# Second attention: value products as three one-pass products of high and low parts

## The reference, cut to what matters

```python
q = _apply_axial_rope(_rmsnorm(q, q_norm), rope)      # 512 x 8 x 128
k = _apply_axial_rope(_rmsnorm(k, k_norm), rope)      # 512 x 2 x 128
out = _blocked_attention([q], [k], v, GQA_HEAD_DIM ** -0.5)
...
s = jnp.einsum('bqkgd,bskd->bkgqs', qp, kp)
p = jax.nn.softmax(s * scale, axis=-1).astype(v.dtype)
return jnp.einsum('bkgqs,bskd->bqkgd', p, v)          # the value products
```

## Time and profile before

| | |
|---|---|
| median of 3 runs | 2506.69 us (2506.29 to 2506.73) |
| the profiled execution | 2506.91 us, span 2505.1 us |
| TensorE busy in the span | 2477.2 us (99%) |
| DVE, ACT, POOL busy | 1015.4, 1084.5, 1413.0 us |
| the second attention's phase 1 | about 2000 to 2080 us of the span |
| value products of phase 1 (L1678) | 64 records, 29.9 us busy |

### The profile page before, as it was taken

How to read it: one execution, slowest core, us unless ns; L and a number is a source line. 1 busy time by engine, 2 the same in 40 slices (tenths; PEclk the granted TensorE clock), 3 DMA queues, 4 the chain that set the end, 5 groups by cost and what they waited for, 6 DMA issues and landing times.

```text
span 2505.1 us, 36572 instructions
## 1 busy us (share of the span) xinstructions
PE 2477.2 (99%) x12648; PEld 2020.0 (81%) x12648; DVE 1015.4 (41%) x2240; ACT 1084.5 (43%) x1866; POOL 1413.0 (56%) x1100
## 2 busy tenths in 40 slices
PE   9999999999999999999999999999999999999999
PEld 7888888888888888888867688888888767888887
DVE  7567532125586652115676522111025672211100
ACT  6346552226447554225467433333144573333321
POOL 6445765566644765557734545566466264555553
PEclk9999999999999999999999999999999999999999
DMA  5312113324212112333320123333343112332332
GB/s 197 101 60 85 44 51 94 101 80 143 92 60 85 60 39 89 96 98 117 120 68 26 34 76 101 100 92 100 94 124 102 51 34 68 95 98 92 101 95 73
DMA packets 62367, 215.12 MB, mean 86 GB/s; under 512 B 7312, under 2 KB 10512, under 8 KB 61840
## 3 DMA queue, kind: packets, MB, share of 16 engines
q1 hardware_dynamic: 62224, 213.28, 27.4%
HBM read 211.16 MB, written 2.10 MB: 85 GB/s over the span
## 4 chain that ended last, share of the span: by engine, by line
PE 92%; DVE 3%; ACT 2%; POOL 1%; issue 1%; DMA 0%; SPq 0%; ACTq 0%; DVEq 0%; POOLq 0%
PE bank L873 24%; PE bank L875 24%; PE bank L874 24%; PE pair L1678 2%; PE pair L873 2%; PE pair L874 2%; PE pair L875 2%; PE bank L1743 1%; PE bank L1711 1%; PE pair L1505 1%; PE bank L1268 1%; PE pair L1281 1%; POOL wl L2596 1%; PE bank L1239 1%; PE bank L1219 1%
## 5 line engine op out<-in xcount | busy, mean ns | idle before, releaser
L2596 POOL TENSOR_TENSOR wl<-raw,wh 128x512 fp32r<-128x512 f32 x750 | 1002.5, 1360 | 867.5 <-ACT wh L2547 286.9
L873 PE MATMUL bank<-hh,wh 128*128 128x512 f32 x1600 | 632.1, 395 | 1.1 <-ACT rv L1961 0.9
L875 PE MATMUL bank<-hh,wl 128*128 128x512 f32 x1600 | 623.5, 390 | 0.0
L874 PE MATMUL bank<-hl,wh 128*128 128x512 f32 x1600 | 622.8, 389 | 0.0
L873 PEld LDWEIGHTS bank<-hh,wh 128*128 128x128 f32 x1600 | 300.5, 188 | 63.5 <-ACT rv L1961 2.7
L875 PEld LDWEIGHTS bank<-hh,wl 128*128 128x128 f32 x1600 | 300.3, 188 | 63.3
L874 PEld LDWEIGHTS bank<-hl,wh 128*128 128x128 f32 x1600 | 300.7, 188 | 59.5
L2547 ACT CAST wh<-raw 128x1024 fp32r<-128x1024 f32 x120 | 125.5, 1048 | 254.0 <-PE pair L875 140.2
L1927 ACT CAST wh<-raw 128x1024 fp32r<-128x1024 f32 x104 | 109.1, 1050 | 117.9 <-PE bank L875 92.0
L873 PE MATMUL bank<-wh,hh 128*128 128x512 f32 (+2 forms) x352 | 138.8, 394 | 2.6 <-DVE hl L2940 1.2
L2210 ACT CAST wh<-raw 128x1024 fp32r<-128x1024 f32 x84 | 86.8, 1049 | 122.1 <-PE bank L875 107.1
(11 more groups left out here) (514 smaller groups left out, 4712.3 us busy)
## 6 DMA issues: line engine op xcount, KB each, us to landing
raw<-stream SPq DMA_DIRECT2D x384, 512.0 KB, 3.6
mraw<-memin SPq DMA_DIRECT2D x3, 1024.0 KB, 5.6
par<-params SPq DMA_DIRECT2D x2, 1124.5 KB, 9.1
out<-xT SPq DMA_DIRECT2D x8, 256.0 KB, 2.0
con<-consts SPq DMA_DIRECT2D x1, 1540.0 KB, 14.9
xT<-xin SPq DMA_DIRECT2D x2, 512.0 KB, 4.6
xT<-xin SPq DMA_DIRECT2D x1, 1024.0 KB, 8.5
con<-consts SPq DMA_DIRECT2D x1, 512.0 KB, 3.2
```

Of the source, the lines that this page charges most:

```text
L873: mm(o, ah, bh, start=start, stop=False)
L874: mm(o, ah, bl, start=False, stop=False)
L875: return mm(o, al, bh, start=False, stop=stop)
L2596: m = TT(wl[slot][:, c], raw[slot][:, c], wh[slot][:, c].bitcast(F32), ALU.subtract)
```

## The change

Each turned bank is now written twice: ACT writes its high part (PTh, F32R) for all 32 tiles, and DVE the low part (PTl) for all 32, as the bank minus the high part, so DVE waits for ACT. The value tiles are split in the same way, in steps 1 (ACT, vh) and 2 (DVE, vl, in place over v). Each value product becomes a call of `three`. A turned bank is free when the low part is made. The low parts of the features of query group B move to another place, since the second set of turned probabilities needs theirs.

```diff
@@ -283,6 +283,11 @@
 
 
 PT_RING = 3
+
+
+def high_parts(m):
+
+    return 4 + NT + m + 1
 
 
 def mix_bank(e):
@@ -684,7 +689,7 @@
             b["msum"] = sb("msum_1", [P, N_MEM], at=r1 + 44 * KB_)
             b["q"] = tiles_at("q", 8, a2, dt=F32R)
             b["k"] = tiles_at("k", 2, a2 + 16 * KB_, dt=F32R)
-            b["ql"] = tiles_at("qAl", 4, r1 + 8 * KB_, dt=F32R) + tiles_at("qBl", 4, hreg + 8 * KB_, dt=F32R)
+            b["ql"] = tiles_at("qAl", 4, r1 + 8 * KB_, dt=F32R) + tiles_at("qBl", 4, r1 + 32 * KB_, dt=F32R)
             b["kl"] = tiles_at("kl", 2, a2 + 44 * KB_, dt=F32R)
             b["v"] = tiles_at("v", 4, a2 + 20 * KB_, (P, 256))
             b["qm"] = tiles_at("qm", 4, a2 + 24 * KB_)
@@ -693,8 +698,11 @@
             b["mP"], b["mPT"] = tiles_at("mP", 4, r1, (P, N_MEM)), tiles_at("mPT", 2, r1 + 4 * KB_)
             b["ra"], b["rb"] = (sb(f"{n}_1", [P, T], at=a2 + at * KB_) for n, at in (("ra", 40), ("rb", 42)))
             b["P"] = tiles_at("P", 4, hreg + 16 * KB_)
-            b["PT_sets"] = [sb(f"PT_1_{x}", [P, NT, T], at=at) for x, at in enumerate((a2 + 32 * KB_, hreg))]
-            b["PT"], b["PT_odd"] = ([s_[:, kb] for kb in range(NT)] for s_ in b["PT_sets"])
+            b["PTh"] = [sb(f"PTh_1_{x}", [P, NT, T], F32R, at=at) for x, at in enumerate((a2 + 32 * KB_, hreg))]
+            b["PTl"] = [sb(f"PTl_1_{x}", [P, NT, T], F32R, at=at) for x, at in enumerate((a2 + 24 * KB_, hreg + 8 * KB_))]
+            b["vl"] = tiles_at("vl", 4, a2 + 20 * KB_, (P, 256), F32R)
+            b["vh"] = tiles_at("vh", 4, hreg + 26 * KB_, (P, 256), F32R)
+            b["PT"] = b["PT_odd"] = b["mPT"] * 2
             b["qraw"] = sb("qraw", [P, T], at=hreg + 24 * KB_)
     ah = sb("ah", [P, FF, T], F32R, at=r1)
     al = sb("al", [P, FF, T], F32R, at=r1 + 44 * KB_)
@@ -1667,12 +1675,17 @@
                         if a + (4 if len(phases) == 2 and phase else 0) >= back and value_bank(i, phase, a) in outs:
                             pe.wait_ge(t["mix_lo"].sem, t["mix_lo"].at(a0 + a - back + 1))
                         if (i, phase) == (1, 1):
-                            pe.wait_ge(t["pt_a"].sem, t["pt_a"].at(copies_before(1, a + 1)))
-                            pe.wait_ge(t["pt_d"].sem, t["pt_d"].at(copies_before(1, a + 1)))
+                            pe.wait_ge(t["pt_a"].sem, t["pt_a"].at(high_parts(4 * a + 3)))
+                            pe.wait_ge(t["pt_d"].sem, t["pt_d"].at(high_parts(4 * a + 3)))
                         for kb in blocks:
                             copied, first = (t["pt_a"], 0) if kb < nk // 2 else (t["pt_d"], nk // 2)
                             if (i, phase) != (1, 1):
                                 pe.wait_ge(copied.sem, copied.at(copies_before(phase, a) + kb - first + 1))
+                            if (i, phase) == (1, 1):
+                                c = slice((a // 4) * P, (a // 4 + 1) * P)
+                                x = three(bk[value_bank(i, phase, a)], b["vh"][kb][:, c], b["vl"][kb][:, c], b["PTh"][a % 2][:, kb],
+                                          b["PTl"][a % 2][:, kb], kb == 0, kb == nk - 1)
+                                continue
                             vv = (b["mv"][kb][:, a * P:(a + 1) * P] if phase == 0 else
                                   b["v"][kb][:, a * P:(a + 1) * P] if i == 0 else b["v"][kb][:, (a // 4) * P:(a // 4 + 1) * P])
                             x = mm(bk[value_bank(i, phase, a)], vv, pts[a % 2][kb][:, :], start=(kb == 0), stop=(kb == nk - 1))
@@ -1732,8 +1745,7 @@
                                 pe.wait_ge(t["mix_lo"].sem, t["mix_lo"].at(4))
                         pe.wait_ge(t["p"].sem, t["p"].at(m0 + m + 1))
                         if (i, phase) == (1, 1) and m >= PT_RING:
-                            copied = t["pt_d" if (m - PT_RING) % 2 else "pt_a"]
-                            pe.wait_ge(copied.sem, copied.at(copies_before(1, 0) + (m - PT_RING) // 2 + 1))
+                            pe.wait_ge(t["pt_d"].sem, t["pt_d"].at(high_parts(m - PT_RING)))
                         elif qt == 0 and a0 + a:
                             pe.wait_ge(t["pt_a"].sem, t["pt_a"].at(copies_before(phase, a)))
                             pe.wait_ge(t["pt_d"].sem, t["pt_d"].at(copies_before(phase, a)))
@@ -2484,6 +2496,9 @@
                             if step == 16:
                                 take_root("qA")
                                 take_root("qB")
+                        elif step == 1:
+                            for x in range(NT):
+                                A(b["vh"][x][:, :], b["v"][x][:, :], ACT.Copy).then_inc(t["pt_a"].sem, 1)
                         elif step in QB_TURNS:
                             feature("qB", QB_TURNS.index(step), bk[3])
                         elif step in (12, 16, 20, 24):
@@ -2503,11 +2518,10 @@
                     pp = b["mP"] if phase == 0 else b["P"]
                     if turn and (i, phase) == (1, 1):
                         m, a, qt = turn
-                        if m % 2 == 0:
-                            act.wait_ge(t["flipped"].sem, t["flipped"].at(m0 + m + 1))
-                            if a >= sets:
-                                act.wait_ge(t["o"].sem, t["o"].at(a0 + a - sets + 1))
-                            A(b["PT_sets"][a % 2][:, :, qt * P:(qt + 1) * P], b4[m % PT_RING], ACT.Copy).then_inc(t["pt_a"].sem, 1)
+                        act.wait_ge(t["flipped"].sem, t["flipped"].at(m0 + m + 1))
+                        if a >= sets:
+                            act.wait_ge(t["o"].sem, t["o"].at(a0 + a - sets + 1))
+                        A(b["PTh"][a % 2][:, :, qt * P:(qt + 1) * P], b4[m % PT_RING], ACT.Copy).then_inc(t["pt_a"].sem, 1)
                     elif turn and turn[2] == NT - 1:
                         m, a, qt = turn
                         act.wait_ge(t["flipped"].sem, t["flipped"].at(m0 + m + 1))
@@ -3677,6 +3691,10 @@
                         if phase:
                             if step == 2:
                                 own.end()
+                                for x in range(NT):
+                                    dve.wait_ge(t["pt_a"].sem, t["pt_a"].at(4 + x + 1))
+                                    V.tensor_tensor(b["vl"][x][:, :], b["v"][x][:, :], b["vh"][x][:, :].bitcast(F32),
+                                                    ALU.subtract).then_inc(t["pt_d"].sem, 1)
                             if step in QB_TURNS:
                                 low_part("qB", QB_TURNS.index(step), bk[3])
                             return
@@ -3720,11 +3738,12 @@
                                         ALU.mult).then_inc(t["bias"].sem, 1)
                     if turn and (i, phase) == (1, 1):
                         m, a, qt = turn
-                        if m % 2:
-                            dve.wait_ge(t["flipped"].sem, t["flipped"].at(m0 + m + 1))
-                            if a >= sets:
-                                dve.wait_ge(t["o"].sem, t["o"].at(a0 + a - sets + 1))
-                            V.tensor_copy(b["PT_sets"][a % 2][:, :, qt * P:(qt + 1) * P], b4[m % PT_RING]).then_inc(t["pt_d"].sem, 1)
+                        dve.wait_ge(t["pt_a"].sem, t["pt_a"].at(high_parts(m)))
+                        if a >= sets:
+                            dve.wait_ge(t["o"].sem, t["o"].at(a0 + a - sets + 1))
+                        c = slice(qt * P, (qt + 1) * P)
+                        V.tensor_tensor(b["PTl"][a % 2][:, :, c], b4[m % PT_RING], b["PTh"][a % 2][:, :, c].bitcast(F32),
+                                        ALU.subtract).then_inc(t["pt_d"].sem, 1)
                     elif turn and turn[2] == NT - 1:
                         m, a, qt = turn
                         dve.wait_ge(t["flipped"].sem, t["flipped"].at(m0 + m + 1))
```

## The result

The changed kernel takes 2510.88 us (2510.2 to 2512.14), against 2506.71 us (2506.2 to 2507.24) for the kernel before on the same chip: a ratio of 1.0017, interval 1.0011 to 1.0023. So 4.17 us were lost; the forecast was 2511.3 us, a loss of 4.6. The prediction put at some 5.0 us what a measurement of this kernel can tell from no change; with 22 runs of each kernel a loss of 4.17 us could be told from none.

What follows compares the result with a forecast made beforehand. TensorE bound the kernel before; after the change, ACT and DVE chains would: 5.6 us late at score tile 30, less 1.0 back in value halves, +4.6 on 2506.69 gives 2511.3 us; range 2503.5 to 2515.0.

Steps and rivals of the forecast that it cites:

- The chains decide: Second attention: handovers through ACT's and DVE's in-order queues, not TensorE's work, set the pace; +4.6 us, chance 0.50.
- periods with a cast: Steps 10 to 30, four score tiles each, with one granule cast on ACT: 8.48 us against 7.96 before.
- Rival B: Second attention: handoffs are hidden and TensorE stays the bound; -1.6 us, or -5.1 if the start is absorbed; chance 0.25.
- The v copies: Start of phase, ACT: four copies between the first exponentials take 1.4 us, of which about 1.0 us delays later work.
- DVE's subtractions of v "cost nothing": Start of phase: DVE's four subtractions lie in its wait for the last memory head's mixh, adding nothing; uncovered, about 1.4 us.
- The loops: Steps 3 to 9: three two-step chains through DVE and ACT grow from 3.87 to 4.49 us, +0.62 each.
- r(10): DVE's row maximum of step 10, after the start and three loops: 2.86 us late, at 2027.29.
- T(30): TensorE's turning of score tile 30: 5.6 us late, then 1.0 us back in three shorter value halves.
- Rival C: DVE, second attention: instructions run end to end, 0.08 us more per handover; +8.0 us, 2514.7 us; chance 0.20.
- Rival D: TensorE value products: one-pass products do not follow each other by 0.23 us; at 0.28, +5.6 us, 2512.3; chance 0.05.
- The value half and TensorE's need: TensorE, two of a head's four key blocks: 1.38 us, 0.32 less; four steps then need 7.32 us.
- the case with 0.50: The forecast itself: ACT and DVE chains set the second attention's pace, +2 to +7 us; 0.20 of it above +5.0.

Runs made afterwards that it cites:

- the best order: Changed kernel with casts earlier, reciprocal before low part, v copies and subtractions spread, and low parts of steps 3, 5, 7 deferred one step: 2504.88 us, ratio 0.9993.

## Why the prediction was right, by its steps

- **"The chains decide"** held. TensorE idles (40.28 us busy, against the 43.73 of the earlier trace rows), and periods with a cast are 8.44 us with three products, one product and plain ones. Rival B is excluded by this: with one product TensorE's work is far below any chain, and the time does not follow it.
- **The v copies.** ACT's four took 1.23 us from the first start to e(2) (2008.35 to 2009.58), forecast 1.36. r(3) was 0.91 us late, forecast 1.0. By the formula of the Trainium skill (VectorE: DVE Perf Modes, The TRN2 errata) one copy is an estimate of 0.40 us; the trace agrees, with 0.41. Neighbours overlap by some 0.1 us, so four of them take 1.23 and not 1.6.
- **DVE's subtractions of v "cost nothing"** held barely, and not by the sum I made. They took 2.27 us to mixl (2008.80 to 2011.07), where four of the undisturbed ones, of 0.41 us, make 1.6 at most; with mixh's start at 2010.34 and its 0.63, mixl could have started at 2010.97, so 0.1 us shows. That the cost stayed this small was luck: the cover was just long enough.
- **The loops** took 4.47 us, forecast 4.49; r(10) was 2.71 us late, forecast 2.86.
- **Periods with a cast** took 8.44 us, forecast 8.48, through the cast, the copy and the low part as in the timeline above. The one without took 7.73 us, forecast 7.54: there T(26) waits for its division, and the low part behind it is a little late.
- **T(30)** was 5.43 us late, forecast 5.6, and 1.04 came back, forecast 1.0. The small terms above make up the difference: 0.09 less at r(3), 0.06 less in the loops, 0.16 less in four periods, 0.19 more in the fifth, and a few hundredths in the rest. So the fifth period's error offset part of the others.
- **Rival C** is excluded. In the earlier trace rows t lasts 0.21 us and the copy starts 0.13 us after it; after the change it is the same (0.14, from 2041.65 to 2041.79), and the next instruction still starts 0.6 us into the low part's 0.69 (2044.24 to 2044.85 above, behind the new wait of 0.85 us). End to end, six such handovers of 0.08 us would have made the periods some 0.5 us longer than the forecast's 8.48. The Trainium skill (VectorE: DVE Perf Modes, The DRAIN you can't avoid) has the next operation wait until the pipeline is empty; the same page lets an instruction that is not held start earlier, and the trace agrees with that, new waits or not.
- **Rival D** is excluded: the products start 0.23 us apart (2044.45, 2044.68, 2044.91 and 2045.15).
- **The value half and TensorE's need** held. In the kernel with cast and reciprocal moved, turnings on TensorE are

```profile
2043.53 0.60 PE L1755 MATMUL bank<-con,P 128*128 128x128 f32 x4
...
2044.65 0.60 PE L1755 MATMUL bank<-con,P 128*128 128x128 f32 x4
...
2047.18 0.60 PE L1755 MATMUL bank<-con,P 128*128 128x128 f32 x4
```

1.12 us apart without a value half and 2.53 with one, with no wait between. So a half costs 1.41 us, forecast 1.38, and four steps with two halves need 7.30 us, forecast 7.32. The kernels with cast and reciprocal moved take 7.47, by DVE's own queue, so at most 0.17 us a period, 0.9 us in five, are still to be had there. The rest of what the best order loses is at the start, where r(9) comes at 2022.45 in its profile, 17.94 us behind r(0); in the kernel before these are 16.92 us. The 1.02 us are three loops of 4.21 us for 3.87, the price of ACT's additional copy between the two exponentials.

The chances: the case with 0.50 came, near the centre of its +2 to +7 us, and with 0.17% within the bound of 0.2%.

## What to carry to other kernels

When work is moved off the busiest engine, compare not only the engines' sums but the chain of handovers through their in-order queues over one full period of the order; here every engine had slack and the period still grew by 0.5 us. A new wait costs what stands in front of it on the other engine: look for the longest instruction there (here the cast, 1.04 us) and put it where nothing waits. Before delaying an instruction, ask who waits for it: with a single output bank, mixl put off by a step made the periods 8.44 us, where cast and reciprocal moved without it give 7.47.

## What the hardware showed that was not expected

The subtraction of v reads two operands from SBUF on DVE, and takes 0.41 us alone, but up to 1.26 beside POOL's division. The views of its line and of POOL's division, in the kernel after and then in the two kernels with single subtractions (ns: least, median, most; first and last start):

```profile
L3696 DVE TENSOR_TENSOR vl<-v,vh x4: 414/456/1257, 2008.8 to 2010.7; 128x256 fp32r<-128x256 f32 x4
L3696 DVE TENSOR_TENSOR vl<-v,vh x1: 1257/1257/1257, 2009.2 to 2009.2; 128x256 fp32r<-128x256 f32 x1
L2797 POOL TENSOR_TENSOR P<-P,soft x1: 1222/1222/1222, 2009.0 to 2009.0; 128x512 f32<-128x512 f32 x1
```

```profile
L3702 DVE TENSOR_TENSOR vl<-v,vh x4: 894/895/896, 2013.1 to 2025.0; 128x256 fp32r<-128x256 f32 x4
...
2012.72 1.04 POOL L2802 TENSOR_TENSOR P<-P,soft 128x512 f32<-128x512 f32 x1 [0.46 <-DVE soft L3762]
...
2013.15 0.89 DVE L3702 TENSOR_TENSOR vl<-v,vh 128x256 fp32r<-128x256 f32 x1
```

```profile
L3702 DVE TENSOR_TENSOR vl<-v,vh x4: 416/416/896, 2013.0 to 2024.0; 128x256 fp32r<-128x256 f32 x4
...
2011.93 1.04 POOL L2802 TENSOR_TENSOR P<-P,soft 128x512 f32<-128x512 f32 x1
```

The first two fences are of kernels where the subtraction starts during a division, the third of one where it starts as the division ends (2012.96 against 2011.93 + 1.04 = 2012.97): 0.42 us. Three of its four start so; the fourth starts at 2023.95, inside a division that began at 2023.53, and is the one of 0.90. In the second, the division ends at 2013.76 and the subtraction at 2014.04, 0.28 later; in the first, POOL's second division ends at some 2010.2 (2007.97 + 2.22), and DVE's second subtraction, begun at 2009.2, at 2010.46, again 0.27 later. So the one that came second did most of its work only when the first was done; POOL too, whose second division lasts 1.22 for 1.04 us. DVE's low parts, which read a PSUM bank and one SBUF tile, last 0.67 to 0.69 us beside the same divisions, so no such delay shows in them.

The Trainium skill states this (SBUF — State Buffer, SBUF: two separate sides): of a DVE instruction with two SBUF inputs and a GpSimd instruction that reads SBUF, the one that starts first takes a shared pair of ports for the whole instruction, and the other is blocked. These rows agree, but the profile shows the blocked one as begun and long, not as late. I had not applied it to the v subtractions. It is why they took 2.27 us where at most 1.6 would have been needed, and why in the kernel with v spread in pairs the two loops with them grew to 5.1 us.
